# A hybrid pool/RWKV-7 layer: the slots of its round re-sequenced, matrix pieces grouped in threes, and work around the round moved

## The chip, the cores and the metric

One core of one Trainium2 chip runs the kernel. The time is the device time of one execution in microseconds (us). TensorE (PE) multiplies matrices, VectorE (DVE) and ScalarE (ACT) do elementwise work, GpSimd (POOL) does elementwise work and masks, SyncE (SP) issues most transfers. Each engine runs its own list of instructions in order and waits on semaphores.

## The reference, cut to what matters

One layer on 512 tokens of width 1024, all in float32:

```python
mod = silu(c) @ w_ada + b_ada            # sh1, sc1, gt1, sh2, sc2, gt2
h = x * (1 + sc1) + sh1
p = h @ w_in                             # p_pool, p_rwkv, p_gate
y_pool = pool_branch(p_pool, ...)        # means over 2, 4, 8, 16 tokens, a mix, @ w_pool_up
y_rwkv = rwkv7_branch(p_rwkv, ...)       # below
mixed = (g_pool * y_pool + g_rwkv * y_rwkv) @ w_out
x = layer_norm(ALPHA * x + (1 + gt1) * mixed)
f = square(relu((x * (1 + sc2) + sh2) @ w_ff1)) @ w_ff2
x = layer_norm(ALPHA * x + (1 + gt2) * f)
# rwkv7_branch, for each of 16 heads of width 64 and each token in turn:
state = state * decay + (state @ -kk) * (kk * a) + v * k
o = state @ r;  o = layer_norm(o) + bonus * v;  o = o * gate;  y_rwkv = o @ w_rwkv_up
```

## The kernel before

Every large product is made in three terms: weights and activations are split into a high part (ACT, `split_hi`) and the remainder (POOL, `split_lo`), and PE adds high by high, high by low and low by high. A weight chunk of 1024 by 128 columns takes 24 matmuls of 512 columns. `w_hi` and `w_lo` are a ring of two chunks until the rounds are done, so a chunk is split only when the product two chunks before is finished.

**Prologue.** SP loads sixteen tiles of `w_ada`, the token tile, fifteen rows of parameters and the first two weight chunks. DVE adds the tiles up weighted by silu(c) (`acc`, L973 to L976), PE turns the sums into columns (L1404) and `mod` is their value. Then `hf`, its high part and its low part are made tile by tile (L995, L648, L998, L560) and PE does the first five chunks (L1426).

**Rounds.** The recurrence is done in chunks of 64 tokens as matrix products (with an inverse made by squaring), four heads at a time, so in four rounds (`QUADS`). `it` runs from -1 to 4: round `it` works on four heads (`work`), prepares the next four (`prep`, not in `it` 3 and 4) and finishes the four before (`tail`, `it` 1 to 4). A round has 27 slots (`SLOTS`). In each slot every engine does what `slot(it, s)` names, in order. PE's small products (64 by 64 blocks) go to three PSUM sets in the order of `PE_ORDER`, set = place in the list modulo 3; `wait_set_free` makes a product wait until the one before it in its set has been read. Between them PE does pieces of the weight products that go on all the while: a piece is four matmuls (`gemm_piece`), a chunk six pieces, `PER_SLOT` says how many follow the small products of a slot, 36 to a round, in 26 of the 27 slots.

The names that matter below. AT0, AT1, TV, AD0, AD1, A2T, A4, A4T, D1, KR0, KR1, A8T, D2, W0, D, K, HD0, HD1, V1, K2, TT, AP, MR, N, OI are steps of the recurrence; S1 to S6 carry the state from chunk to chunk, one in each of the slots 21 to 26, each waiting for DVE's addition of the one before (L1241). `lora`, `norm` and `inv` (twice a round, 0 and 1) prepare the next heads: ACT's `lora_tanh`, the square root of `norm_root` (L702), DVE's `norm_inverse` (L1075, L1078), PE's `inverse_norm` (L1564), DVE's `unit_keys`, `keys`, `scaled_reads`, `scaled_writes`. The tail normalises `O` over each head: mean (L1152), centring (L1161), square (ACT, L787), sum (L1166), root (ACT, L791), division (L1187), then PE turns it (`yT`), ACT scales it into `y` (L823), DVE adds the bonus (L1210) and multiplies by the gate (L1212, `y_ready`), for which PE makes `gate` (L1591, L1592). ACT needs a table load of its own between square roots and exponentials or tanh. In each round eight more tiles of `w_ada` come through ACT's queue to one place (`ada_tile`), at the slots `ADA_LOADED`, and DVE adds them up at the end of the slots `ADA_USED` (L1249); PE makes `mod` of the sum in the next round. An ACT issue waits until DVE has used up the tile before.

**After the rounds.** The last two gate products of group 3 and the pool mixing (L1765) run while the up-projections' first chunk is loaded, then the up-projections, gates, `w_out`, the first layer norm, four quarters of the feed-forward, the last layer norm.

Of the kernel before, what the change touches and what calls it, by code (L numbers as in the profile page):

```python
# [5 lines left out]
P = 128  # L6
# [7 lines left out]
def build(nc, x, c, w_ada, b_ada, w_in, mu_shift, pool_mix, pool_scale, w_pool_up, w0, w_decay_up, a0,  # L14
# [30 lines left out]
    with ctx:  # L45
# [157 lines left out]
        def over16(m):  # L203
# [5 lines left out]
                    "D1", "KR0", "KR1", "A8T", "D2", "W0", "inv0", "bonus", "D", "lora1", "K", "HD0", "HD1", "yT", "norm1", "gate",  # L209
# [223 lines left out]
        def _(sp):  # L433
# [11 lines left out]
            for q in range(2 * KT):  # L445
# [30 lines left out]
            for k in range(K_UP, K_FF + 2 * KT):  # L476
# [21 lines left out]
        def _(pool):  # L498
# [99 lines left out]
            for k in range(K_UP, K_H2):  # L598
# [1298 lines left out]
```

## Time and profile before

| | |
|---|---|
| time, 3 runs | 1108.73 us median, 1107.64 to 1111.6 |
| profiled execution | 1109.78 us, its span 1108.0 us |
| mean granted TensorE clock | 0.957 of full |
| busy, share of the span | PE 91%, DVE 47%, ACT 37%, POOL 37% |
| prologue, up to the first wide matmul | 0 to 42.4 us |
| rounds -1, 0, 1, 2, 3, 4 begin at | 71.4, 118.9, 210.7, 312.6, 415.1, 511.4 us |
| rounds end | 534.5 us |
| first feed-forward product begins | 726.9 us |

The span runs from the first to the last instruction; the execution's own time is a little longer. Busy PE includes the time in which it runs at the lower of its two clocks.

### The profile page before, as it was taken

What the parts mean: (1) busy time and instruction counts of PE and PEld (TensorE: products, weight loads), DVE (VectorE), ACT (ScalarE), POOL (GpSimd) and SP (SyncE); (2) the same over time, 40 slices, a digit from 0 to 9 for tenths busy, and PEclk for the clock granted to TensorE, in tenths of its full rate; (3) what the DMA queues carried; (4) which work ended last, traced back from release to release, by engine and by line L of the source; (5) the groups of instructions that cost most, each with busy time, mean ns of one, the idle gap of its engine ahead of it and who ended that gap; (6) DMA issues with size and microseconds to landing.
All of it is one profiled execution on the core that took longest, in us unless ns stands there. A gap on an engine that the chain in (4) does not pass through costs nothing.

```text
span 1108.0 us, 25424 instructions
## 1 busy us (share of the span) xinstructions
PE 1008.7 (91%) x10997; PEld 799.2 (72%) x10997; DVE 522.0 (47%) x620; ACT 408.5 (37%) x496; POOL 407.6 (37%) x236
## 2 busy tenths in 40 slices
PE   1898999879988999899899999889999999999992
PEld 1676777666766677677588888768888888888881
DVE  6636578558846775753332155846112112112217
ACT  0345354336234522433532233475224224214311
POOL 7333412402320141123454453436444444444422
PEclk9798999889999998899999999979999999999996
DMA  9322333312432342333334443304323332333201
GB/s 373 101 77 62 97 101 89 91 57 85 114 87 64 98 116 61 96 85 96 116 97 116 135 125 110 93 20 122 106 85 98 105 95 87 102 95 88 84 1 76
DMA packets 153641, 108.08 MB, mean 98 GB/s; under 512 B 5395, under 2 KB 145601, under 8 KB 153537
## 3 DMA queue, kind: packets, MB, share of 16 engines
q1 hardware_dynamic: 143729, 83.46, 25.7%
q10 hardware_dynamic: 9808, 23.08, 7.1%
q8 instruction: 84, 1.38, 0.5%
q14 instruction: 20, 0.16, 0.0%
HBM read 100.23 MB, written 2.10 MB: 92 GB/s over the span
## 4 chain that ended last, share of the span: by engine, by line
PE 76%; DVE 13%; ACT 3%; DMA 2%; issue 2%; POOL 1%; SPq 1%; ACTq 0%; DVEq 0%; POOLq 0%
PE set L1742 23%; PE bank L1742 20%; PE bank L1445 13%; PE set L1499 3%; PE set L1487 3%; PE set L1511 3%; PE set L1523 2%; PE bank L1426 1%; DVE y L1249 1%; PE bank L1844 1%; DVE Q L1020 1%; DMA ptab<-in_mu_shift_dram 1%; DVE Q L1039 1%; PE set L1564 1%; PE set L1534 1%
## 5 line engine op out<-in xcount | busy, mean ns | idle before, releaser
L552 POOL TENSOR_TENSOR w_lo<-w_raw,w_hi 128x1024 fp32r<-128x1024 f32 (+2 forms) x87 | 201.3, 2313 | 443.7 <-ACT w_hi L633 403.6
L608 POOL TENSOR_TENSOR w_lo<-w_raw,w_hi 128x1024 fp32r<-128x1024 f32 x48 | 115.8, 2412 | 145.6 <-ACT w_hi L924 145.5
L661 ACT ACTIVATE Q<-set 128x1024 f32<-128x1024 f32 x56 | 57.4, 1025 | 155.1 <-PE set L1499 83.6
L1445 PE MATMUL bank<-h_hi,w_hi 128*128 128x512 f32 x256 | 110.7, 432 | 0.9 <-issue 0.6
L1445 PE MATMUL bank<-h_hi,w_lo 128*128 128x512 f32 x256 | 108.0, 422 | 0.7 <-issue 0.7
L1445 PE MATMUL bank<-h_lo,w_hi 128*128 128x512 f32 x256 | 108.0, 422 | 0.0
L633 ACT ACTIVATE w_hi<-w_raw 128x1024 fp32r<-128x1024 f32 (+2 forms) x75 | 75.4, 1006 | 81.4 <-PE set L1742 43.5
L924 ACT ACTIVATE w_hi<-w_raw 128x1024 fp32r<-128x1024 f32 x60 | 63.7, 1061 | 110.7 <-PE bank L1742 53.9
L1340 DVE TENSOR_TENSOR f<-t 128x512 f32<-128x512 f32 x32 | 26.4, 825 | 125.5 <-ACT t L933 125.2
L1742 PE MATMUL set<-y_hi,w_hi 128*128 128x512 f32 x192 | 76.1, 396 | 0.0
L1742 PE MATMUL bank<-h_hi,w_hi 128*128 128x512 f32 x192 | 75.8, 395 | 0.0
L1742 PE MATMUL bank<-h_hi,w_lo 128*128 128x512 f32 x192 | 75.3, 392 | 0.0
L1742 PE MATMUL bank<-h_lo,w_hi 128*128 128x512 f32 x192 | 75.2, 392 | 0.0
L1742 PE MATMUL set<-y_lo,w_hi 128*128 128x512 f32 x192 | 75.2, 391 | 0.0
L1742 PE MATMUL set<-y_hi,w_lo 128*128 128x512 f32 x192 | 75.1, 391 | 0.0
L1445 PEld LDWEIGHTS bank<-h_hi,w_lo 128*128 128x128 f32 x256 | 50.5, 197 | 16.5 <-issue 6.2
L1445 PEld LDWEIGHTS bank<-h_hi,w_hi 128*128 128x128 f32 x256 | 50.6, 198 | 15.7 <-issue 4.6
L1445 PEld LDWEIGHTS bank<-h_lo,w_hi 128*128 128x128 f32 x256 | 50.8, 198 | 12.0 <-issue 2.3
L1742 PE MATMUL bank<-y_hi,w_hi 128*128 128x512 f32 x128 | 50.8, 397 | 0.0
L1742 PE MATMUL bank<-y_hi,w_lo 128*128 128x512 f32 x128 | 50.2, 392 | 0.0
L1742 PE MATMUL bank<-y_lo,w_hi 128*128 128x512 f32 x128 | 50.1, 392 | 0.0
L1499 PEld LDWEIGHTS set<-Q 64*64 64x64 f32 x2560 | 41.6, 136 | 11.1 <-issue 9.9
(325 smaller groups left out, 2026.9 us busy)
## 6 DMA issues: line engine op xcount, KB each, us to landing
w_raw<-in_w_ff_dram SPq DMA_DIRECT2D x64, 512.0 KB, 3.9
w_raw<-in_w_in_dram SPq DMA_DIRECT2D x46, 512.0 KB, 3.9
y<-in_w_ada_dram ACTq DMA_DIRECT2D x32, 512.0 KB, 3.8
ada<-in_w_ada_dram SPq DMA_DIRECT2D x16, 512.0 KB, 9.4
w_raw<-in_w_rwkv_up_dram SPq DMA_DIRECT2D x8, 512.0 KB, 3.9
w_raw<-in_w_out_dram SPq DMA_DIRECT2D x8, 512.0 KB, 3.8
xtok<-in_x_dram SPq DMA_DIRECT2D x4, 512.0 KB, 9.7
Q<-Q ACTq DMA_DIRECT2D x16, 128.0 KB
```

The source lines that it names most:

```text
L552: link(pool.tensor_tensor(part_of(k, w_lo), part_of(k, w_raw), part_of(k, w_hi).bitcast(F32), ALU.subtract), "lo_ready")
L608: again(pool.tensor_tensor(part_of(k, w_lo), part_of(k, w_raw), part_of(k, w_hi).bitcast(F32), ALU.subtract), "lo_ready")
L633: link(act.activation(part_of(k, w_hi), part_of(k, w_raw), ACT.Copy), "hi_ready")
L661: link(act.activation(by_half(tile), psum_flat(set_of(name)), ACT.Copy), "act_kept")
L924: link(act.activation(part_of(k, w_hi), part_of(k, w_raw), ACT.Copy), "hi_ready")
L1340: link(dve.tensor_tensor(f3[:, :], r[:, :], r[:, :], ALU.mult))
L1445: mm = pe.matmul(o, w, hx, start=(m == 0), stop=(m == 3 * KT - 1))
L1487: mm = pe.matmul(ps[C * q:C * q + C, p, c * C:(c + 1) * C], by_head(left, p, q, c), by_head(right, p, q, c - back), start=(m == 0), stop=( ...
L1499: mm = pe.matmul(ps[N * p:N * p + N, q, c * C:(c + 1) * C], by_pair(left, p, q, c), by_pair(right, p, q, c), start=(m == 0), stop=(m == le ...
L1511: mm = pe.matmul(ps[C * q:C * q + C, p, 2 * c * C:2 * (c + 1) * C], by_head(left, p, q, HC * h + c), two_blocks(x, z, rows, q, HC * h + c) ...
L1523: mm = pe.matmul(ps[N * p:N * p + N, q, 2 * c * C:2 * (c + 1) * C], by_pair(left, p, q, HC * h + c), two_blocks(x, z, rows, p, HC * h + c) ...
L1742: mm = pe.matmul(o, w[chunks[k][1]][:, kt, :], hx[:, kt, :], start=(kt == 0 and m == 0), stop=(kt == kts - 1 and m == 2))
```

## The change

Nothing is computed in another way. What moves:

- `PER_SLOT` puts the 36 pieces of a round as ten groups of three and six single ones; round -1 has a list of its own (`FIRST_SLOTS`). The small products do not change their order but for `gate`, which goes ahead of `yT`; so `gate` takes the set of number 2, `yT` 0, `norm1` 1.
- The tail: `mod` is added at slot 2 and not after AT1's masks at slot 3; square, variance and root go from slots 4 and 5 to 8 and 9, the division from 8 to 10, and the squares go to the place of `At` and not `b7`.
- `scaled_writes(n, 1)` goes from slot 20 to slot 18, ahead of the additions of MR0 and MR1.
- The eight tiles of `w_ada` come at other slots and through two places, `y` and the block `c1`.
- Prologue: parameters two to a tile, chunk loads ahead of the last two tiles of `w_ada`, the parameters' work and the first half of `mod` between DVE's two sums, and the first two chunks' products side by side, tile by tile.
- After the rounds: the first two up-projection chunks and the mixing weights are loaded earlier, `split_hi(K_UP)` comes later on ACT; at the first layer norm DVE centres the next tile before it sums up, POOL's last split goes behind the low parts, and DVE makes the first low part.

```diff
-                    "D1", "KR0", "KR1", "A8T", "D2", "W0", "inv0", "bonus", "D", "lora1", "K", "HD0", "HD1", "yT", "norm1", "gate",
+                    "D1", "KR0", "KR1", "A8T", "D2", "W0", "inv0", "bonus", "D", "lora1", "K", "HD0", "HD1", "gate", "yT", "norm1",
...
-        ADA_LOADED = (1, 5, 8, 11, 14, 17, 19, 21)
-        ADA_USED = (4, 7, 10, 13, 16, 18, 20, 26)
+        ADA_LOADED = (1, 5, 7, 9, 11, 12, 14, 15)
+        ADA_USED = (4, 8, 10, 11, 13, 14, 16, 18)
+        def ada_tile(kt):
+            return flat_blocks(c1) if kt in (2, 4, 6) else y[:, KT - 2:KT, :].rearrange("p g t -> p (g t)")
+        def ada_before(kt):
+            return (0, 1, 1, 2, 3, 4, 5, 6)[kt]
...
-        PER_SLOT = [1, 1, 1, 2, 2, 1, 1, 2, 1, 1, 1, 2, 1, 1, 0, 2, 1, 3, 3, 1, 2, 1, 1, 1, 1, 1, 1]
+        PER_SLOT = [0, 3, 0, 3, 3, 0, 3, 0, 3, 0, 3, 0, 3, 0, 0, 3, 0, 3, 3, 0, 1, 1, 1, 1, 1, 1, 0]
         LAST_SLOTS = [2, 2, 2, 1, 1, 1, 1, 1, 1] + [0] * 18
+        FIRST_SLOTS = [0, 3, 0, 3, 0, 0, 3, 0, 3, 0, 0, 0, 3, 6, 0, 3, 0, 3, 3, 3, 3, 0, 0, 0, 0, 0, 0]
...
-                if 2 <= q < 2 + len(rows):
-                    tab, at, src = rows[q - 2]
+                for tab, at, src in rows[2 * (q - 2):2 * (q - 1)] if q >= 2 else ():
...
+                if q in (2 * KT - 4, 2 * KT - 3):
+                    load_chunk(sp, q - (2 * KT - 4))
...
-            sp.wait_ge(sem("y_ready"), QUADS)
+            wait_made(sp, "O", QUADS)
+            load_chunk(sp, K_UP)
+            wait_made(sp, "yT", QUADS)
...
+            load_chunk(sp, K_UP + 1)
+            sp.wait_ge(sem("y_ready"), QUADS)
...
-            for f in range(KT):
+            for f in range(1, KT):
...
+            split_lo(K_H2 - 1)
...
+                if s == 9 and tail:
+                    act.wait_ge(sem("o_var"), it)
+                    link(act.activation(gn[:, 2, :], gn[:, 1, :], ACT.Sqrt), "o_std")
+                if s == 8:
...
+                    if tail:
+                        act.wait_ge(sem("centred"), it)
+                        link(act.activation(flat_blocks(At), flat(O), ACT.Square), "o_squared")
...
+                    if it or ada_before(kt):
+                        act.wait_ge(sem("ada2_used"), KT * it + ada_before(kt))
+                    if kt == 2:
+                        wait_made(act, "D1", it)
...
+                if q == KT:
+                    modulation_in()
...
+                    if s == 18 and prep:
+                        scaled_writes(n, 1)
+                if s == 2 and tail:
...
+                    link(dve.tensor_tensor(mod[:, cols], pset[set_of("mod")][:, 0, 0:KT], params[:, cols], ALU.add), "mod2")
...
+                if s == 9 and tail:
+                    dve.wait_ge(sem("o_squared"), it)
+                    link(dve.tensor_reduce(gn[:, 1, :], blocks(At), AX_X, ALU.add))
...
+                if f == 1:
+                    dve.wait_ge(sem("h2_hi"), 1)
+                    link(dve.tensor_tensor(h_lo[:, 0, :], f1[:, :], h_hi[:, 0, :].bitcast(F32), ALU.subtract), "h2_lo_first")
...
+            modulation_columns(0, bank[1])
...
+            modulation_columns(1, bank[7])
+            for f in range(4, 6):
+                turn_x(f)
...
+            for kt in range(KT):
...
+                for k in range(2):
+                    for m in range(3 * kt, 3 * kt + 3):
...
                 if s == 13:
                     if tail:
+                        out_gate(it)
                         pe.wait_ge(sem("o_normed"), it)
                         to_heads("yT", it, [(O, IB)])
                     if prep:
                         norm(it, 1)
-                if s == 14 and tail:
-                    out_gate(it)
```

## Rows read from the trace of the kernel before

**Rows 1.** The page: busy us (share of the span) and instructions of each engine

```profile
PE 1008.7 (91%) x10997; PEld 799.2 (72%) x10997; DVE 522.0 (47%) x620; ACT 408.5 (37%) x496; POOL 407.6 (37%) x236
```

**Rows 2.** Waits of PE, whole span: who waited for whom, us in total, times, longest

```profile
PE set L1487 <- ACT norms L702: 7.5, 2, 3.7
...
PE set L1564 <- DVE inverse L1078: 6.2, 2, 4.7
PE set L1487 <- DVE mod L1151: 6.0, 3, 2.1
PE set L1534 <- DVE Q L1241: 4.4, 2, 2.8
...
PE set L1844 <- POOL h_lo L603: 3.9, 1, 3.9
...
PE set L1499 <- DVE O L1187: 2.2, 1, 2.2
```

**Rows 3.** Rounds -1 to 3: length, busy us of PE, PEld, DVE, ACT, POOL, granted clock, DMA

```profile
71.40:118.90 47.50, 42.78 (x205) 32.64 (x203) 29.27 (x38) 22.70 (x28) 17.29 (x8) 0.93 0.26 70
118.90:210.70 91.80, 83.93 (x1921) 65.06 (x1920) 61.93 (x70) 41.31 (x47) 25.92 (x11) 0.96 0.36 101
210.70:312.60 101.90, 92.48 (x2064) 70.61 (x2063) 69.45 (x82) 44.12 (x51) 24.18 (x10) 0.97 0.32 88
312.60:415.10 102.50, 92.82 (x2065) 70.87 (x2064) 69.39 (x81) 44.05 (x51) 24.10 (x10) 0.97 0.31 86
415.10:511.40 96.30, 89.34 (x2005) 68.92 (x2004) 56.82 (x76) 33.95 (x37) 19.72 (x8) 0.93 0.33 91
```

**Rows 4.** The same columns, a stretch just behind a wait in round 1

```profile
227.30:230.70 3.40, 3.40 (x8) 2.40 (x8) 0.14 (x1) 1.02 (x1) 0.00 (x0) 0.51 0.24 57
```

**Rows 5.** PE in order of time, three pieces in round 1: start, us, operation

```profile
278.86 0.50 PE L1445 MATMUL bank<-h_hi,w_hi 128*128 128x512 f32 x1
279.20 0.40 PE L1445 MATMUL bank<-h_lo,w_hi 128*128 128x512 f32 x1
...
281.53 0.39 PE L1445 MATMUL bank<-h_hi,w_lo 128*128 128x512 f32 x1
281.85 1.16 PE L1499 MATMUL set<-Q 64*64 64x64 f32 x64
```

**Rows 6.** Round 1 in order of time: from yT to the gated y

```profile
269.94 1.59 ACT L823 ACTIVATE y<-set,params 128x512 f32<-128x512 f32 x2 [0.67 <-PE set L1499]
...
271.54 1.28 ACT L702 ACT_TABLE_LOAD   x1
...
273.56 1.22 DVE L1210 TENSOR_TENSOR y<-y,xvb 128x1024 f32<-128x1024 f32 x1
```

**Rows 7.** Round 1 in order of time: DVE and ACT ahead of lora_tanh(1)

```profile
239.99 1.22 DVE L1166 TENSOR_REDUCE gn<-Q 128x16 f32<-128x1024 f32 x1
...
258.58 1.23 DVE L1194 TENSOR_TENSOR xvb<-set,xvb 128x1024 f32<-128x1024 f32 x1 [0.55 <-PE set L1582]
...
262.86 1.29 DVE L1249 SCALAR_TENSOR_TENSOR y<-y,derived 128x1024 f32<-128x1024 f32 x1
...
264.69 0.69 ACT L694 ACTIVATE sg<-set,derived 128x512 f32<-128x512 f32 x1 [2.29 <-DVE y L1249]
```

**Rows 8.** First layer norm in order of time

```profile
717.12 2.34 POOL L552 TENSOR_TENSOR w_lo<-w_raw,w_hi 128x1024 fp32r<-128x1024 f32 x1 [7.76 <-ACT w_hi L633]
...
717.83 1.65 DVE L1316 TENSOR_SCALAR small<-small 128x4 f32<-128x4 f32 x1
```

**Rows 9.** Prologue in order of time

```profile
29.51 6.83 PE L1404 MATMUL bank<-ones_col,acc 128*128 128x1 f32 x32
...
31.28 1.06 ACT L633 ACTIVATE w_hi<-w_raw 128x1024 fp32r<-128x1024 f32 x1 [27.58 <-DMA w_raw<-in_w_in_dram]
...
33.06 1.06 ACT L633 ACTIVATE w_hi<-w_raw 128x1024 fp32r<-128x1024 f32 x1 [0.72 <-DMA w_raw<-in_w_in_dram]
```

**Rows 10.** After the rounds, in order of time

```profile
545.42 1.06 ACT L633 ACTIVATE w_hi<-w_raw 128x1024 fp32r<-128x1024 f32 x1 [7.88 <-DMA w_raw<-in_w_rwkv_up_dram]
```

More of the change, by code:

```diff
@@ L1163, in slot @@
                         decay_sums(n, 0)
-                if s == 5 and tail:
-                    dve.wait_ge(sem("o_squared"), it)
-                    link(dve.tensor_reduce(gn[:, 1, :], blocks(b7), AX_X, ALU.add))
-                    link(dve.tensor_scalar(gn[:, 1, :], gn[:, 1, :], 1.0 / N, GN_EPS, ALU.mult, ALU.add), "o_var")
                 if s == 6:
@@ L1183, in slot @@
                         keep_plus_one(b5, "A8T", "A8T", it)
-                    if tail:
-                        dve.wait_ge(sem("o_std"), it)
-                        link(dve.reciprocal(gn[:, 3, :], gn[:, 2, :]))
-                        link(dve.tensor_tensor(blocks16(O), blocks16(O), gn[:, 3, :].unsqueeze(2).to_broadcast([P, 16, N]), ALU.mult), "o_normed")
                 if s == 9:
@@ L1229, in slot @@
                 if s == 20 and prep:
-                    scaled_writes(n, 1)
                     for q in range(2):
@@ L1301, in _, with first_centre @@
             link(dve.tensor_copy(sum1, res[:, 0, :]))
-            for n in range(1, KT):
+            def first_centre(n):
                 dve.wait_ge(sem("res_ready"), n + 1)
                 link(dve.tensor_tensor(res[:, n, :], res[:, n, :], m0[:, :], ALU.subtract))
+            first_centre(1)
+            for n in range(1, KT):
                 take_product(n)
+                if n < KT - 1:
+                    first_centre(n + 1)
                 if n < KT - 1:
@@ L1390, in turn_x, with modulation_columns @@
                 mm.then_inc(sem("x_turned"), 1)
-            pe.wait_ge(sem("x_in"), 16 * TB)
-            for f in range(4):
-                turn_x(f)
+            def modulation_columns(half, o):
+                pe.wait_ge(sem("ada_used"), KT * (half + 1))
+                for f in range(KT):
+                    mm = pe.matmul(o[:, f:f + 1], acc[:, half, f * P:(f + 1) * P], ones_col[:, :], start=True, stop=True)
+                mm.then_inc(sem("mod_done"), 1)
+            pe.wait_ge(sem("ones_ready"), 1)
+            modulation_columns(0, bank[1])
             pe.wait_ge(sem("params_in"), 16 * 15)
@@ L1399, in _ @@
             mm.then_inc(sem("param_cols"), 1)
-            pe.wait_ge(sem("ones_ready"), 1)
-            for half in range(2):
-                pe.wait_ge(sem("ada_used"), KT * (half + 1))
-                for f in range(KT):
-                    mm = pe.matmul(bank[1][:, 8 * half + f:8 * half + f + 1], acc[:, half, f * P:(f + 1) * P],
-                                   ones_col[:, :], start=True, stop=True)
-            mm.then_inc(sem("mod_done"), 1)
-            for f in range(4, KT):
+            pe.wait_ge(sem("x_in"), 16 * TB)
+            for f in range(4):
+                turn_x(f)
+            modulation_columns(1, bank[7])
+            for f in range(4, 6):
                 turn_x(f)
@@ L1414, in terms_of @@
                 return in_bank(k)[0:width, :], w[slot_of(k)][:, kt, 0:width], hx[:, kt, :]
-            for k in range(5):
+            pe.wait_ge(sem("lo_ready"), 2)
+            for kt in range(KT):
+                pe.wait_ge(sem(("h_lo_by_dve", "h_lo_by_pool")[kt % 2]), kt // 2 + 1)
+                for k in range(2):
+                    for m in range(3 * kt, 3 * kt + 3):
+                        o, w, hx = terms_of(k, m)
+                        mm = pe.matmul(o, w, hx, start=(m == 0), stop=(m == 3 * KT - 1))
+                    if kt == KT - 1:
+                        mm.then_inc(sem("w_used"), 1)
+                if kt < 2:
+                    turn_x(6 + kt)
+            for k in range(2, 5):
                 pe.wait_ge(sem("lo_ready"), k + 1)
```

95 lines of the change are left out of this document (44 added, 51 removed).

## The prediction

> **What bounds the kernel now.** The page comes first: PE is busy 91% of the span, all others under half [rows 1]. So only two things can shorten it, PE's idle time and what PE is busy with beyond its work: starts of segments, and time at the lower clock. PE's waits, one by one, say where the idle time is [rows 2]: two waits of 3.7 us for the square root of `norm_root`, two for the inverse norm (4.7 in round -1, 1.5 in round 0), three of 2.1 for `mod`, two in the state steps (2.8 in round 0, 1.6 in round 1), 3.9 ahead of the feed-forward, 2.2 for the last `yT`. The windows by round give the sums that the change has to be set against, with the granted clock: 0.93 in rounds -1 and 3, 0.96 to 0.97 between [rows 3]. A stretch behind one of the waits runs at 0.51, the lower of the two levels, for 3.4 us and gives half of its work [rows 4]; so a wait of over 2 us mostly costs 1.7 us more than itself. In round 3, 0.93 over 96.3 us is 14% of it at the lower clock, 6.7 us lost; in round -1 3.3.
>
> I price the change by walking through each slot in the new order with the durations of before. All sums are against the profiled execution's 1109.8 us; the median of the runs is 1.05 us under it.
>
> **Pieces in threes.** A segment of twelve matmuls takes 2.99 us: 0.34 to its second, 0.32 from its last to the next small product, and (281.53 - 279.20) / 10 = 0.233 between [rows 5]. So each segment costs (0.34 + 0.32 - 2 x 0.23) = 0.2 us beyond its matmuls. A round has 16 segments in place of some 25: 9 x 0.2 = 1.8 us less, 7 us over four rounds.
>
> **Round -1.** The list puts six pieces between `norm1` and `inv1`, where one stood. A piece is 0.93 us, so five more (4.7) cover the 4.7 wait, and the low clock behind it goes (3.3). The six added to covers elsewhere are taken from the end, where POOL has to make its two scaled blocks before TB; that comes out even. With 1 us kept back: **-7**.
>
> **Round 0.** The state-step wait came from DVE's `scaled_writes`, `rt` products and an `ada` tile ahead of L1241. `scaled_writes` goes to slot 18, where DVE has three pieces of slack. 2.8 goes to about 1.6 (ACT's flips still delay the projection at slot 22, and one piece less stands ahead of it), the low clock behind it goes (0.04 x 91.8 = 3.7), segments 1.8; against it, `norm1` and `inv1` now stand without a piece between, so the 1.5 wait grows by a piece to 2.2 or 2.4: **-5** after some small waits (BR0 for TB's copy, HD1 for the tanh).
>
> **Rounds 1 and 2.** Gone: 2.1 for `mod` (it is added before the masks), 3.7 for `norm_root` (the tail's root no longer stands ahead of it), segments 1.8, and the low clock behind both, 0.03 x 102 = 3.1. New, and the heart of this prediction:
> - *HD1.* ACT's `lora_tanh(1)` already waited 2.29 for DVE to use up an `ada` tile [rows 7]. DVE's stretch from the bonus product to the end of that tile is 264.15 - 258.58 = 5.6 us. Into it come the sum (1.22 and a small one), the reciprocal and the division (the size of the sum): 3.0 us, so 8.6. Bonus itself comes two pieces later after PE's A8T. And ACT has a root in slot 9, so tanh needs a table load of 1.28 [rows 6] that it did not need before. HD1 shares its set with `lora1`: PE reaches HD1 about 17 us after A8T, the tanh is done after 21: a wait of 4.
> - *inv1.* `gate` now has set 2, and the next in set 2 is `inv1`, so PE waits there for `y_ready`, not only for the inverse. From the end of `yT`: 0.2, two scalings 1.59, table load 1.28, root 0.2, inverse 0.4, two DVE passes of 1.22 [rows 6]: 6.2 us. PE has only `norm1`, 0.9, to put against it: a wait of 5.3.
> - Behind these two waits 1.7 us of clock each, and in round 1 the state-step wait goes from 1.6 to 2.5.
> Sum: round 1 gives up 10.7 and takes 14 to 15: **+4**; round 2, where slot 22 has no projection, **+1**.
>
> The Trainium skill (ScalarE: Activation LUTs, What ACT_TABLE_LOAD costs) speaks against the change here: it puts a switch of function sets at 2.66 us, 1.28 of load and 1.38 of drain. The row shows 1.28, and ACT's next instruction starts right behind it; I take the row. By the page the two waits would be about 1.4 us longer each, in two rounds some 5 us on the sum.
>
> **Round 3** has no preparation, so neither new wait. The waits for `mod` and for the variance ahead of KR go, two or three low stretches with them. Small content and 36 pieces come to 80 us, waits for D's copy behind the root 1.8, for y's scaling before V1 1.9, hiccups 1.5: 85 against 96.3 [rows 3], **-11**.
>
> **Round 4 and after.** `gate` (4.1 us of PE) covers the chain to the division: the wait of 2.2 [rows 2] and the slow stretch behind it go, -3. The first up-projection chunk no longer comes at 545.4 [rows 10]; ACT's queue gets past it, and two waits at the pool mixing go: -2. Together **-5**.
>
> **Prologue.** The work for `mod`'s first half leaves the end of the chain: half of 6.83 [rows 9], -3.4. But the chunk loads now stand ahead of the last two tiles; one chunk lands 1.8 us behind the other [rows 9], so the last tile lands 3.6 later. And POOL then splits both chunks while DVE still adds tiles: beside a split of 2.34 a DVE instruction on four columns took 1.65 [rows 8], so each split may hold DVE for up to 2.3. That gives 0 to +4 at `hf`. The two chunks side by side start 1 to 2 us earlier and wait less for tiles, but both end together, so the third chunk's copy, split and low part (2 us) are no longer covered. Bounds 0 to +5; I take **+3.5**, since the splits fall on the additions.
>
> **First layer norm.** POOL's split is no longer ahead: 1.65 to 0.17, -1.5 [rows 8]; the first low part by DVE -0.7. **-2.5** with the clock. Reordering the centring leaves the same operations ahead of the last sum: nothing.
>
> Sum: -7 - 5 + 4 + 1 - 11 - 5 + 3.5 - 2.5 = -22, so 1088 for the profiled execution, and **1087** for the median.
>
> **The rivals.** *The new waits are half what I make them* (DVE ahead of my walk, PE behind it, each hiding the other): half of twice (4 + 5.3 + 3.4) = 13 us off, 1075. For it: the old DVE was idle a third of the round [rows 3]. Against: both are chains of fixed lengths.
> *Most is lost again:* the chains that I find in two rounds bite in rounds 0 and 3 too, or collisions of POOL with DVE on the new path, a few at 2.3 each: +12, 1099.
> *Nothing comes of it,* because round 3 keeps its waits (11) and the prologue loses 5 or more: 1107.
> *Slower.* With pieces in threes there are long stretches of 64-column products alone, up to 6 us. Should these be granted the lower clock, each costs 1.7 us in 3.4. It decides from about 15 such stretches more than I count, three to four a round: then 1115. In its favour, the first tiles of `mod` in round 3 are followed by the low level with hardly a wait ahead. Against: rounds 1 and 2 have such stretches of 4 us now at a mean clock of 0.97. The Trainium skill (TensorE: Matmul & The Clock Gate, HAM oscillation) says that a kernel can lose the clock again at every wait of a loop; the low stretch behind a wait agrees [rows 4].
>
> **How the numbers follow.** The forecast's own range is 1080 to 1096, 0.58. Half waits 0.18; mostly lost 0.12; nothing 0.06; slower 0.06. Under 1073 and over 1103 I leave 0.2 in all, most of it above. A difference of 0.5%, 5.5 us, is what a measurement tells from none. Faster: 0.58 + 0.18 + 0.12 - 0.02 = 0.86; same 0.07; slower 0.07.
>
> **What would show it.** In rounds 1 and 2 a wait of about 4 at HD1 for ACT's tanh and one of about 5 at L1564 for DVE's gate multiplication (L1212 of before), no wait at TV or D1; no wait at `inv1` in round -1; round 3 near 85 us; rounds 1 and 2 not shorter. Wrong it would be if DVE's work of slots 9 and 10 were held further by collisions, if the clock fell in stretches without a wait, or if the chunk loads cost the prologue more than 5.

## The result: 0.34% slower, where 2% faster was forecast

The changed kernel takes 1113.61 us (median of 20 runs, 1106.94 to 1118.47) beside 1108.74 us for the kernel before in the same runs: a ratio of 1.0034, 95% interval 1.0019 to 1.0048. The forecast was 1087, range 1073 to 1103. The profiled execution took 1113.02 us, its span 1111.3.

Busy time of each engine, from the page of the changed kernel:

```profile
PE 996.6 (90%) x10997; PEld 800.9 (72%) x10997; DVE 523.9 (47%) x621; ACT 413.8 (37%) x500; POOL 402.9 (36%) x235
```

PE has the same instructions and is busy 12 us less than before [rows 1]; that is the part that worked. It idles 15 us more, so the gain is more than spent on waiting. Its waits, in the changed kernel (who waited for whom, us in total, times, longest):

```profile
PE bank L1426 <- DVE acc L1007: 13.4, 1, 13.4
PE set L1426 <- DVE acc L1007: 13.4, 1, 13.4
PE set L1604 <- DVE y L1236: 10.7, 2, 5.3
PE set L1539 <- issue: 8.9, 10, 1.9
PE set L1563 <- ACT aa_odd L707: 7.6, 3, 3.7
PE set L1539 <- DVE Q L1064: 6.2, 3, 2.5
PE set L1883 <- DVE h_lo L1357: 3.3, 1, 3.3
PE set L1574 <- DVE Q L1264: 3.2, 2, 1.9
...
PE set L1527 <- issue: 2.7, 3, 1.1
PE set L1539 <- DVE O L1220: 2.5, 1, 2.5
...
PE set L1527 <- ACT y L836: 1.8, 1, 1.8
```

L1604 is `inverse_norm`, L1563 HD1, L1574 the state steps, L1426 the columns of `mod` in the prologue. Against [rows 2]: the waits for `mod` and for `norm_root` are gone, and the one of 4.7 in round -1 is 1.6. In their place stand the two that were forecast, 3.7 at HD1 and 5.3 at `inv1`, in each of rounds 1 and 2. And there is a line that was not forecast: waits on "issue", for nothing that the profile shows. All of these on PE, in any line, sum to 14.0 us in 16 pauses; before they summed to 7.9 in ten.

Not all of them are of one kind. Number everything that PE's trace records, in order: matmuls, weight loads, semaphore and register instructions. Before, all ten pauses stand at numbers that leave 193 to 195 when divided by 256. In the changed kernel twelve of the 16 leave 193 or 194; these sum to 10.0 us. The other four (1.87, 0.80, 0.80 and 0.45 us) stand elsewhere, and each ends within 0.1 us of the end of an operation by which ACT or DVE writes `Q`; I read them as waits for data that the profile did not name. So the pauses that repeat every 256 instructions grew by some 2 us over the whole kernel, and not by 6; in round 3 alone they grew from 1.3 to 5.8.

By round (us, busy of PE, PEld, DVE, ACT, POOL, granted clock, DMA share and GB/s; rounds -1, 0, 1, 2, 3, and last the stretch behind the wait at HD1 in round 1):

```profile
75.40:117.30 41.90, 39.93 (x205) 30.58 (x203) 28.77 (x38) 22.72 (x28) 16.48 (x7) 1.00 0.29 79
117.30:205.30 88.00, 80.47 (x1917) 64.65 (x1918) 62.34 (x69) 41.36 (x47) 25.38 (x12) 0.98 0.36 103
205.30:314.70 109.40, 93.45 (x2064) 73.59 (x2064) 68.96 (x81) 46.72 (x53) 23.79 (x10) 0.92 0.30 84
314.70:420.20 105.50, 90.74 (x2068) 71.84 (x2068) 68.23 (x80) 46.63 (x53) 24.10 (x10) 0.95 0.28 79
420.20:516.90 96.70, 85.31 (x2012) 68.08 (x2008) 60.13 (x76) 34.74 (x39) 19.57 (x8) 0.96 0.33 92
257.60:264.40 6.80, 5.47 (x40) 4.39 (x41) 5.67 (x6) 4.31 (x5) 0.00 (x0) 0.50 0.31 102
```

Round -1 lost its low clock (0.93 to 1.00) and 5.6 us, round 0 lost 3.8 us. Round 1 is 7.5 longer and round 2 3.0 longer, both at a lower mean clock than before (0.92 and 0.95 beside 0.97 [rows 3]), for the clock falls to its lower level behind each of the new waits. Round 3, where 11 us were to be gained, is as long as before.

### The profile page after: what moved, and what is told of

Same layout as the page of the kernel before. It is cut to its first block, busy times and chain, and to the rows that moved or that the text cites. A ratio compares the mean times of both kernels' runs of the same rounds, so it can differ in the third digit from the quotient of the medians.

```text
span 1111.3 us, 25426 instructions
## 1 busy us (share of the span) xinstructions
PE 996.6 (90%) x10997; PEld 800.9 (72%) x10997; DVE 523.9 (47%) x621; ACT 413.8 (37%) x500; POOL 402.9 (36%) x235
## 3 DMA queue, kind: packets, MB, share of 16 engines
q8 instruction: 84, 1.38, 0.5%
## 4 chain that ended last, share of the span: by engine, by line
PE 45%; DVE 5%; ACT 1%; issue 0%; POOL 0%; DVEq 0%; ACTq 0%; POOLq 0%
PE set L1781 22%; PE bank L1781 20%; PE bank L1883 1%; DVE G L1327 1%; DVE aa L1335 1%; DVE t L1312 1%; PE set L1883 1%; DVE xt L1404 1%; DVE xt L1406 1%; DVE G L1316 0%; PE set L1845 0%; PE set L1862 0%; DVE stat L1364 0%; PE set L1769 0%; DVE O L1220 0%
## 5 line engine op out<-in xcount | busy, mean ns | idle before, releaser
L1485 PE MATMUL bank<-h_lo,w_hi 128*128 128x512 f32 x256 | 103.3, 404 | 0.0
L1485 PE MATMUL bank<-h_hi,w_lo 128*128 128x512 f32 x256 | 102.5, 400 | 0.0
L1781 PE MATMUL set<-y_hi,w_hi 128*128 128x512 f32 x192 | 75.8, 395 | 0.4 <-POOL w_lo L563 0.4
L1781 PE MATMUL bank<-h_hi,w_lo 128*128 128x512 f32 x192 | 75.5, 393 | 0.0
L1781 PE MATMUL bank<-h_lo,w_hi 128*128 128x512 f32 x192 | 75.4, 393 | 0.0
L1781 PE MATMUL set<-y_lo,w_hi 128*128 128x512 f32 x192 | 75.2, 391 | 0.0
L1539 PE MATMUL set<-Q 64*64 64x64 f32 x2560 | 45.7, 223 | 16.0 <-issue 8.9
```

The lines of the kernel that those rows point to most:

```text
L1485: mm = pe.matmul(o, w, hx, start=(m == 0), stop=(m == 3 * KT - 1))
L1539: mm = pe.matmul(ps[N * p:N * p + N, q, c * C:(c + 1) * C], by_pair(left, p, q, c), by_pair(right, p, q, c), start=(m == 0), stop=(m == le ...
L1781: mm = pe.matmul(o, w[chunks[k][1]][:, kt, :], hx[:, kt, :], start=(kt == 0 and m == 0), stop=(kt == kts - 1 and m == 2))
```

## The experiments

Lengths of the stages in every kernel that computes the layer, from its profiled execution, in us; a stage ends where PE's first product of the next begins. The numbers of a single execution scatter by 2 us a stage and more, since stretches at the lower clock come and go: round 3 of e2_old_slots has a granted clock of 0.91, that of the changed kernel 0.96.

| kernel | prologue | -1 | 0 | 1 | 2 | 3 | 4 | to the feed-forward | rest | ratio to before, 95% interval |
|---|---|---|---|---|---|---|---|---|---|---|
| before | 71.4 | 47.5 | 91.8 | 101.9 | 102.5 | 96.4 | 23.1 | 192.4 | 381.2 | 1 |
| changed | 75.4 | 41.9 | 88.0 | 109.4 | 105.4 | 96.8 | 22.4 | 190.9 | 381.0 | 1.0034 (1.0019 to 1.0048) |
| e1_gate_back | 75.4 | 41.9 | 90.6 | 102.5 | 99.7 | 90.6 | 30.4 | 191.0 | 380.2 | 0.9965 (0.9942 to 0.9988) |
| e2_old_slots | 76.0 | 41.9 | 92.0 | 104.3 | 103.7 | 100.0 | 21.6 | 191.1 | 380.2 | 1.0049 (1.0031 to 1.0066) |
| e3_slots_only | 71.4 | 41.9 | 91.3 | 106.1 | 105.4 | 95.7 | 25.6 | 193.9 | 381.2 | 1.0050 (1.0027 to 1.0073) |
| e5_tanh_first | 75.2 | 41.9 | 95.1 | 105.4 | 102.5 | 97.3 | 22.4 | 193.2 | 381.3 | 1.0034 (1.0017 to 1.0051) |
| e6_chunks_late | 73.5 | 41.9 | 88.9 | 108.8 | 105.7 | 97.2 | 22.4 | 193.2 | 381.3 | 1.0018 (0.9992 to 1.0045) |
| e7_combined | 71.7 | 41.9 | 96.2 | 96.8 | 94.0 | 94.3 | 22.4 | 193.4 | 381.2 | 0.9849 (0.9819 to 0.9879) |
| e8_old_slots_gate_back | 75.8 | 41.9 | 92.6 | 100.5 | 98.1 | 95.8 | 27.3 | 191.1 | 380.2 | 0.9931 (0.9905 to 0.9957) |
| e9_combined_late | 72.2 | 41.9 | 90.7 | 97.9 | 96.8 | 91.7 | 22.5 | 191.8 | 381.3 | 0.9822 (0.9797 to 0.9847) |
| e10_combined_old_slots | 71.8 | 41.9 | 91.3 | 94.1 | 98.2 | 97.2 | 22.1 | 192.3 | 380.8 | 0.9852 (0.9820 to 0.9884) |
| e11_round_4 | 71.7 | 41.9 | 90.6 | 98.2 | 95.8 | 94.2 | 19.1 | 199.9 | 381.2 | 0.9851 (0.9829 to 0.9874) |
| e12_narrow_split | 72.0 | 41.9 | 88.4 | 98.0 | 94.8 | 94.5 | 22.2 | 192.8 | 380.4 | 0.9790 (0.9768 to 0.9813) |

### Gate moved back

```diff
-                    ..., "HD0", "HD1", "gate", "yT", "norm1",
+                    ..., "HD0", "HD1", "yT", "norm1", "gate",
-                        out_gate(it)                     # slot 13
...
+                if s == 14 and tail:
+                    out_gate(it)
```

> The changed kernel with gate behind norm1 again, as before (order of the sets and of the code; the mixing weights are loaded after y_ready again, which that order needs). My theory: the 5.3 us at inv1 in rounds 1 and 2 is the wait for y_ready through the shared set, so it goes, with the low clock behind it: 7 to 8 us less in each of the two rounds; in round 3 the 1.8 us ahead of V1 goes; round 4 gets longer by the cover of the gate product, 4 to 5 us. In sum about 11 us less than the changed kernel, so near 1102. Rival: the chain of ACT and DVE behind yT is the limit whatever stands in the set; then a wait of 4 to 5 us comes back at K2 or at inv1 for the inverse, and the time stays within 3 us of the changed kernel.

Measured: 1105.47 us beside 1109.59 for the kernel before. That is 0.7% under the changed kernel when both are set against before, some 8 us where 11 were expected. The theory holds for the wait: it goes, and does not come back at `inv1` or K2. These rows of the changed kernel show the wait that is undone (start, us, engine, line, operation):

```profile
273.89 0.17 DVE L1095 TENSOR_SCALAR norms<-norms 128x8 f32<-128x8 f32 x1 [9.56 <-ACT norms L714]
274.09 0.20 DVE L1098 RECIPROCAL inverse<-norms 128x8 f32<-128x8 f32 x1
274.33 1.23 DVE L1234 TENSOR_TENSOR y<-y,xvb 128x1024 f32<-128x1024 f32 x1
...
275.59 1.22 DVE L1236 TENSOR_TENSOR y<-y,set 128x1024 f32<-128x1024 f32 x1
...
276.96 1.98 PE L1604 MATMUL set<-ident,inverse 128*64 128x128 f32 x16 [5.34 <-DVE y L1236]
```

The inverse that `inverse_norm` multiplies is there at 274.3, and PE starts only when DVE has read `gate` out of the shared set, at 276.8: 2.5 of the 5.3 us belong to the set alone. With `gate` behind `norm1` its 4.1 us of products cover the rest too, and no wait is left there. The windows of rounds 1, 2 and 3 of this kernel:

```profile
207.90:310.40 102.50, 91.89 (x2065) 72.27 (x2064) 68.77 (x81) 46.73 (x53) 23.03 (x10) 0.95 0.31 88
310.40:410.10 99.70, 89.79 (x2064) 70.66 (x2064) 68.02 (x80) 46.64 (x53) 22.78 (x10) 0.97 0.29 83
410.10:500.70 90.60, 83.54 (x2014) 66.51 (x2013) 59.32 (x76) 34.79 (x39) 19.07 (x8) 0.98 0.36 98
```

They are 6.9, 5.7 and 6.2 us shorter than with `gate` first. For rounds 1 and 2, 7 to 8 each were expected. Round 4 pays 8.0 where 4 to 5 were expected: `yT` waits 6.5 us there, 4.0 more than with `gate` first, and more of the round runs at the lower clock. Of round 3 only the 1.8 at V1 (for ACT's scaling of `y`) were expected; with them go a stretch at the lower clock and, though no piece has moved, 3.1 us of the pauses that repeat with the block of 256 (5.8 to 2.7).

### The slots of before, in the changed kernel

```diff
-        PER_SLOT = [0, 3, 0, 3, 3, 0, 3, 0, 3, 0, 3, 0, 3, 0, 0, 3, 0, 3, 3, 0, 1, 1, 1, 1, 1, 1, 0]
+        PER_SLOT = [1, 1, 1, 2, 2, 1, 1, 2, 1, 1, 1, 2, 1, 1, 0, 2, 1, 3, 3, 1, 2, 1, 1, 1, 1, 1, 1]
```

> The changed kernel with the PER_SLOT of before in rounds 0 to 3 (FIRST_SLOTS kept). My prediction's step: threes save 0.2 us at each of 9 segments in a round, so undoing them costs 7 us, 1121. Rival (instruction supply): the waits that the trace ascribes to nothing ('issue') sum to 14.1 us in the changed kernel and 8.2 before and sit 256 instructions of PE apart, behind long runs of 64-column products; with the old slots they fall back to about 8, so the 7 is mostly cancelled and the time is within 3 us of 1113.6.

Measured: 1113.91 us, ratio 1.0049, no different from the changed kernel's 1.0034. The waits on "issue" fall from 14.0 to 9.9 us. So threes bring nothing here in sum. Where the seven us went that I had put down for them is worked out behind e10_combined_old_slots.

### The new slots alone, in the kernel before

```diff
-        PER_SLOT = [1, 1, 1, 2, 2, 1, ...]
+        PER_SLOT = [0, 3, 0, 3, 3, 0, ...]
...
+        FIRST_SLOTS = [0, 3, 0, 3, 0, 0, 3, 0, 3, 0, 0, 0, 3, 6, 0, 3, 0, 3, 3, 3, 3, 0, 0, 0, 0, 0, 0]
```

> The kernel before with the new PER_SLOT and FIRST_SLOTS alone. Prediction's step: round -1 5.6 to 7 us shorter, rounds 0 to 3 1.8 each, with the waits for mod and norm_root still there: 1096. Instruction supply: round -1 the same, but 'issue' waits of PE rise from 8.2 to about 14: 1101 to 1104. Third: the old tail's waits grow, since the singles that covered them are gone, and it is no faster than before.

Measured: 1113.73 us, 0.5% slower than before, although round -1 gives its 5.6 us. Rounds 1 and 2 grow by 4.2 and 2.9. The first expectation, 1096, is wrong by 18 us; the second, 1101 to 1104, by 10 or more; the third holds. The waits on "issue" are 14.9 us, all at the repeating place in the block, and waits of 2.0 to 2.4 appear at `inv0` in rounds 0, 1 and 2 (its set is that of A8T, which DVE has still to copy); single pieces had covered them.

### Instruction supply by itself

```python
piece(64); narrow(2048)                      # wide: 128x128 by 512 columns; narrow: 64x64 by 64, fp32
for _ in range(8):  piece(12); narrow(192)
for _ in range(24): piece(4);  narrow(64)
for _ in range(4):  piece(12); narrow(384)
```

> The suspected cost by itself: no layer is computed, only 64-column products of 64 rows in fp32, 2048 in a row, then 8 times 12 wide matmuls and 192 narrow ones, then 24 times 4 wide and 64 narrow, then 4 times 12 wide and 384 narrow, with no semaphore between them. Instruction supply: pauses of about 1 us that stand 256 instructions (128 matmuls) apart; in the row of 2048 at nearly every such place, in the 192s at some, with 64s at none or small ones. Rival (no such thing; the 'issue' waits come from semaphores that the trace doesn't show): no pause anywhere, one pitch throughout, and the 8 x (12 + 192) take less than the 24 x (4 + 64) by 16 segment starts of 0.2 us.

A narrow product in fp32 stands as two records, so `narrow(64)` is 128. The kernel ran once. Windows of the four parts (the counts are matmuls, and each has a weight load beside it):

```profile
22.36:138.35 115.99, 66.86 (x4098) 62.64 (x4097) 0.00 (x0) 0.00 (x0) 1.00 0.02 5
138.35:233.20 94.85, 74.00 (x3174) 64.83 (x3168) 0.00 (x0) 0.00 (x0) 1.00 0.02 4
233.20:324.10 90.90, 82.26 (x3175) 66.30 (x3168) 0.00 (x0) 0.00 (x0) 1.00 0.02 5
324.10:417.60 93.50, 61.94 (x3128) 55.86 (x3120) 0.00 (x0) 0.00 (x0) 1.00 0.02 4
```

In order of time, one of the pauses in the first part, and from the page the queue that brings instructions:

```profile
100.33 1.39 PE L53 MATMUL set<-raw 64*64 64x64 f32 x79 [1.64 <-issue]
```

```profile
q8 instruction: 106, 1.74, 1.7%
```

There is no semaphore in these parts. In the first part, behind a first one of 1.12, pauses of 1.36 to 1.91 us stand exactly 128 matmuls apart, which is 256 instructions with the loads, and 106 transfers of 1.74 MB are 16 KB each. The first part takes 116 us for 32 such blocks: **3.6 us for a block**, where the products alone take 2. The second and third part hold the same products, and the second starts 16 segments fewer; a group of four wide ones takes 1.13 us and one of twelve 2.95, so a start costs 0.22 and the second part should be 3.5 us shorter. It is 4.0 longer: bunching costs it 7.5 us of supply. In the third part the pauses are small, 0.1 to 0.8 us but for one of 1.34. All 83 "issue" pauses of this kernel leave 193 when their number is divided by 256, as those of the layer leave 193 to 195: that is why I take the twelve in the changed kernel for the supply of instructions.

The Trainium skill (Runtime: NRT & Kernel Launch, Instruction fetch mechanics) says that instructions come in blocks of 256; the spacing of the pauses agrees. It also says that crossing from one block to the next is mostly hidden. With products as short as these it is not: the row shows 1.64 us.

The rival for "slower" in my prediction, that long stretches of narrow products are granted the lower clock, falls: the first window is 116 us of nothing else at a clock of 1.00.

### ACT's issue out of the way of the tanh

```diff
-        ADA_LOADED = (1, 5, 7, 9, 11, 12, 14, 15)
+        ADA_LOADED = (1, 5, 7, 9, 12, 13, 14, 15)
```

> The changed kernel with two tiles of w_ada issued a slot later (ADA_LOADED 11, 12 become 12, 13), so that ACT no longer stands at an issue, waiting for DVE's use of a tile, ahead of lora_tanh(1). My theory: the tanh then starts right behind the squares and its table load, 2.3 us earlier; the wait at HD1 in rounds 1 and 2 goes from 3.7 to about 1.4 and with it a stretch at the lower clock: 2.3 to 4 us in each of the two rounds, 5 to 8 in sum, about 1107 against 1113.6. Rival: the tanh waits for PE's lora or for the root of the tail whatever ACT issues, then HD1 keeps at least 3 us and nothing changes; or the tile now comes too late for DVE's slot 13 and the wait is found again at inv1.

The rows of the changed kernel that the edit aims at, ACT ahead of the tanh in round 1:

```profile
253.14 0.72 ACT L696 ACTIVATE G<-G,params 128x512 f32<-128x512 f32 x1
255.73 0.34 ACTq L863 DMA_DIRECT2D Q<-in_w_ada_dram  x1
256.17 1.28 ACT L706 ACT_TABLE_LOAD   x1 [2.31 <-DVE y L1272]
257.47 0.69 ACT L706 ACTIVATE sg<-set,derived 128x512 f32<-128x512 f32 x1
258.19 0.69 ACT L707 ACTIVATE aa_odd<-set,derived 128x512 f32<-128x512 f32 x1
...
258.93 1.99 PE L1563 MATMUL set<-Q 64*64 64x128 f32 x32 [3.68 <-ACT aa_odd L707]
```

Measured: 1114.16 us, ratio 1.0034, nothing gained in sum. The mechanism is right: the wait at HD1 is 1.39, and rounds 1 and 2 are 4.0 and 2.9 shorter, although the wait at `inv1` grows from 5.3 to 5.8. The second rival is right too, in round 0, which is 7.1 longer:

```profile
169.84 2.34 POOL L563 TENSOR_TENSOR w_lo<-w_raw,w_hi 128x1024 fp32r<-128x1024 f32 x1 [14.83 <-ACT w_hi L645]
170.08 3.18 DVE L1272 SCALAR_TENSOR_TENSOR y<-Q,derived,y 128x1024 f32<-128x1024 f32 x1 [1.86 <-DMA Q<-in_w_ada_dram]
...
173.76 1.98 PE L1604 MATMUL set<-ident,inverse 128*64 128x128 f32 x16 [5.66 <-DVE inverse L1098]
```

The tile lands late, DVE waits 1.9 us for it and then takes 3.18 us for an addition that takes 1.28 by itself, since POOL splits a chunk beside it; the inverse is queued behind, and PE waits 5.7 for it.

### Chunk loads behind the last tiles

```diff
-                if q in (2 * KT - 4, 2 * KT - 3):
-                    load_chunk(sp, q - (2 * KT - 4))
+            for k in range(RING):
+                load_chunk(sp, k)
```

> The changed kernel with the first two weight chunks loaded behind the last tiles of w_ada, as before, and nothing else. Theory: two of DVE's additions took 3.2 us in place of 1.28 because POOL split the chunks beside them; they come back to 1.3, and hf starts 3.5 to 4 us earlier than 42.1 us. The 3.75 us by which DVE's second sum starts later than before, waiting for the parameters' transposes, stays. 1113.6 becomes about 1110. Rival: the split only moves into the hf products and costs the same there, so the first wide product starts within 1 us of where it does.

Measured: 1112.29 us, ratio 1.0018 (0.9992 to 1.0045), not to be told from the changed kernel, where 3.6 us less were expected. `hf` starts at 40.0 against 42.1, so 2.1 earlier and not 3.5 to 4, for one addition still runs beside a split. In the changed kernel, four additions of which two are held (start, us over all four):

```profile
27.70 9.18 DVE L1007 SCALAR_TENSOR_TENSOR acc<-ada,derived,acc 128x1024 f32<-128x1024 f32 x4
...
29.39 6.41 POOL L563 TENSOR_TENSOR w_lo<-w_raw,w_hi 128x1024 fp32r<-128x1024 f32 x2 [6.44 <-ACT w_hi L645]
```

and in this kernel, two of which one is held:

```profile
31.32 4.75 DVE L1007 SCALAR_TENSOR_TENSOR acc<-ada,derived,acc 128x1024 f32<-128x1024 f32 x2
...
32.64 5.64 POOL L563 TENSOR_TENSOR w_lo<-w_raw,w_hi 128x1024 fp32r<-128x1024 f32 x2 [9.62 <-ACT w_hi L645]
```

DVE's second sum starts at 24 us, some 3.5 later than before, in both: it stands behind the copies of the parameters, whose transposes come on PE behind the columns of the first half.

### Three edits undone or moved, together

Gate first in round 4 alone; the tiles as in e5_tanh_first; the prologue of before.

```diff
-        pe_items = [(name, it) for it in range(-1, QUADS + 1) for name in PE_ORDER if runs(name, it)]
+        pe_items = [(name, it) for it in range(-1, QUADS) for name in PE_ORDER if runs(name, it)]
+        pe_items += [(name, QUADS) for name in ("O", "mod", "gate", "yT")]
...
```

> Gate behind norm1 in rounds 1 to 3 but ahead of yT in round 4, the two tiles of w_ada a slot later, and the prologue of before; the rest as changed. If the terms add up: 1105.5 of the run with gate moved back, 4 less for the prologue, 4 to 8 less in round 4, 5 to 8 less at HD1: about 1090. Rival: waits behind each other, so that what one edit frees is lost at the next place (the state steps, the additions of MR); then 1098 or more.

Measured: 1093.16 us, 1.5% faster than before. Rounds 1 and 2 take 96.8 and 94.0 and round 4 22.4; round 0 keeps the wait of 5.7 us of e5_tanh_first, which the sum of 1090 did not hold. With it, 4 us more than it was before that edit, the terms add up.

### The slots of before, with gate moved back

> The changed kernel with both PER_SLOT and gate as before, so what is left of the round's change is the tail's later steps, the tiles of w_ada and scaled_writes. If threes are worth what the prediction said, it is 7 us slower than the run with gate alone moved back (1105.5), so 1112. If segment starts saved and instruction supply lost cancel, as the run with the old slots alone says, it is within 3 us of 1105.5, with the 'issue' waits of PE summing to less than 10.5 us.

Measured: 1100.82 us, ratio 0.9931, beside 0.9965 for its pair with threes. It comes out below both expectations by 1 to 2 us or more; the "issue" waits sum to 9.1. Threes look 0.3% worse here, though the two intervals (0.9905 to 0.9957 and 0.9942 to 0.9988) still overlap.

### The tiles' use moved as well, and its pair with the slots of before

```diff
-        ADA_LOADED = (1, 5, 7, 9, 12, 13, 14, 15)
-        ADA_USED = (4, 8, 10, 11, 13, 14, 16, 18)
+        ADA_LOADED = (1, 5, 7, 9, 12, 13, 15, 16)
+        ADA_USED = (4, 8, 10, 11, 14, 15, 17, 18)
```

> The combined kernel (1093.2) with DVE's use of the late tiles moved behind the inverse norm too: ADA_LOADED (1, 5, 7, 9, 12, 13, 15, 16), ADA_USED (4, 8, 10, 11, 14, 15, 17, 18). In the combined kernel round 0 took 96.2 us, with 5.7 us at inv1, where DVE stood at slot 13 for a tile that landed late and then ran beside a split of POOL. Theory: that wait goes back to 1.4 us as in the changed kernel, round 0 to about 90, the HD1 waits of rounds 1 and 2 stay at 1.4: near 1087. Rival: tiles used that late push DVE's additions ahead of MR and the state steps, which each wait about 2 us already; then rounds 1 and 2 give the gain back.

> The same with the PER_SLOT of before in rounds 0 to 3: pieces one by one. The pair with gate moved back gave 1105.5 with threes and 1100.8 with the old slots. If threes cost that (starts of segments saved, less instruction supply and covers lost), this is 3 to 5 us faster than its pair, near 1083. If the pair was chance or the covers differ here, both agree within 2 us; if threes gain what I predicted, it is 7 slower.

Measured: 1089.00 and 1093.76 us, ratios 0.9822 and 0.9852. The first is as expected: round 0 goes back to 90.7 with 1.07 at `inv1`. Rounds 0 to 3 of e9_combined_late:

```profile
114.10:204.80 90.70, 82.32 (x1917) 66.32 (x1918) 61.54 (x69) 41.35 (x47) 25.08 (x12) 0.96 0.36 103
204.80:302.70 97.90, 89.04 (x2068) 69.77 (x2066) 68.12 (x81) 46.74 (x53) 22.93 (x10) 0.98 0.32 92
302.70:399.50 96.80, 88.58 (x2064) 70.17 (x2062) 67.32 (x80) 46.64 (x53) 22.74 (x10) 0.98 0.30 86
399.50:491.20 91.70, 82.67 (x2016) 65.35 (x2015) 59.32 (x76) 34.81 (x39) 19.04 (x8) 1.00 0.35 97
```

The second was to be 3 to 5 us faster and is 4.8 slower, its interval overlapping that of the first. So my reading of the pair before it as a fixed price falls. Four pairs now say what threes do to the time in rounds 0 to 3: -0.15% (changed against e2), +0.34% (e1 against e8), -0.30% (e9 against e10), and in the kernel before about +1% (e3, with the 5.6 us of round -1 taken out). The first three are at the edge of what these runs can tell from nothing; the fourth, in a kernel whose waits the single pieces covered, is a loss.

The saving at the starts is there all the same. Two rounds that ran at the full clock from end to end, round 1 of e10_combined_old_slots with single pieces and round 2 of e7_combined with threes:

```profile
204.90:299.00 94.10, 89.11 (x2061) 68.16 (x2060) 67.47 (x81) 46.71 (x53) 23.18 (x10) 1.00 0.33 95
306.70:400.70 94.00, 87.13 (x2070) 68.72 (x2068) 67.88 (x80) 46.62 (x53) 23.51 (x10) 1.00 0.32 90
```

PE is busy 2.0 us less with threes, near the 1.8 forecast, and the round is as long. Over rounds 0 to 3 of the profiled executions (us, threes less singles; the time lost to the lower clock is taken out of PE's busy time by the granted clock of each stretch):

| pair | busy at full clock | PE idle | of it, pauses of the block | lost to the lower clock |
|---|---|---|---|---|
| e3 and before | -5.7 | +13.4 | +7.0 | -1.7 |
| changed and e2 | -7.0 | +11.3 | +3.0 | -4.7 |
| e1 and e8 | -8.2 | +6.4 | -0.4 | -2.0 |
| e9 and e10 | -5.9 | +3.9 | +1.7 | -1.9 |

So threes earn their 6 to 8 us every time, and more idle time spends most or all of it: some of it the supply of instructions, more of it waits that the single pieces had covered. The clock column is within the scatter of single executions.

### Round 4, and the narrow run of slots 18 to 20

```diff
+                if s == 9 and it == QUADS:       # ACT, ahead of the gate and the split of the slot
...
+                    link(act.activation(gn[:, 2, :], gn[:, 1, :], ACT.Sqrt), "o_std")
...
-                if it == QUADS and s in (2, 5):
+                if it == QUADS and s in (2, 10):
```

> The late combined kernel (1089.0) with, in round 4 alone, ACT's root ahead of the gate and split of slot 9, and three of its copies of y behind the root instead of ahead of the squares. In the changed kernel yT of round 4 waits 2.5 us behind gate's 4.1, so the chain from O to the division had grown by 4 us: 1.9 of it are the three copies, 1.7 the gate and the split, the rest a division that ran beside POOL. Theory: that wait goes and the lower clock behind it: 2.5 to 4 us less, 1085 to 1086.5. Rival: the copies are needed by the up-projections soon after, or the root's table load only moves, and the wait stands at the pool mixing: within 1 us of 1089.

Measured: 1094.27 us, ratio 0.9851 beside 0.9822: no gain, where 2.5 to 4 us were expected, and rather a loss. The wait of `yT` is gone and round 4 is 19.1 in place of 22.5, but the stage behind it is 8.1 longer. The rival is right in kind: PE comes to the pool mixing before its weights, whose load follows `y_ready` and one 512 KB chunk:

```profile
523.10 1.22 PE L1801 MATMUL set<-aa,wmix 128*128 128x512 f32 x1 [5.92 <-DMA wmix<-in_pool_mix_dram]
```

```diff
-        PER_SLOT = [..., 0, 3, 3, 0, 1, 1, 1, 1, 1, 1, 0]
+        PER_SLOT = [..., 0, 3, 1, 2, 1, 1, 1, 1, 1, 1, 0]
```

> The late combined kernel with two of the three pieces of slot 18 in slot 19, so that N and OI, 256 64-column records in a row, have eight wide ones between them. Number of pieces, segments and instructions stay but for one start more (0.2 us a round). Instruction supply: in round 3 the pause of 1.9 us in that run goes to under 0.7, in round 1 and 2 the same run's waits (0.7 and 1.6; 2.5, put down to DVE) shrink by 1 to 2 each: 3 to 6 us less, about 1085. Rival: the pause belongs to OI's own inputs and only moves behind the pieces, or MR0 now waits for AP's copies: no gain.

Measured: 1087.31 us, ratio 0.9790 (0.9768 to 0.9813), the fastest of all and 2.1% under the kernel before; the gain over e9_combined_late, 1.7 us or 0.3% where 3 to 6 us were expected, is within the two intervals. The same instruction (the 16,632nd of PE's matmuls and loads) in both, first with N and OI in one run, then with two pieces between them:

```profile
480.75 0.81 PE L1530 MATMUL set<-Q 64*64 64x64 f32 x40 [1.93 <-issue]
```

```profile
479.12 0.81 PE L1530 MATMUL set<-Q 64*64 64x64 f32 x40 [0.40 <-issue]
```

The pause belongs to the place in the list and to the narrow products ahead of it, not to OI's inputs. But the sum of "issue" waits is 14.6 us beside 13.2: other blocks' pauses grew (the one at 410.7 us from 0.4 to 1.75). What one block was spared, another here paid.

## Why the prediction was wrong, step by step

The forecast stood at -22 us against the profiled execution, and +3 came. By its own terms:

- **Round 3, -11, measured +0.4.** This is the step that failed. It said "small content and 36 pieces come to 80 us", waits of 1.8 for D's copy and 1.9 before V1, hiccups 1.5: 85, with nothing for the lower clock. Set beside the traces (us; busy time with the loss to the lower clock taken out):

| | before | forecast | changed |
|---|---|---|---|
| PE busy, at full clock | 82.9 | 80 | 82.1 |
| lost to the lower clock | 6.6 | 0 | 3.2 |
| pauses that repeat with the block of 256 | 1.3 | 1.5 (all hiccups) | 5.8 |
| other idle time | 5.6 | 3.7 | 5.6 |

  Both waits are there: 1.80 at V1, and 1.87 for D's copy, which the profile puts down to "issue" although PE starts just behind the copy:

```profile
467.81 1.02 ACT L673 ACTIVATE Q<-set 128x1024 f32<-128x1024 f32 x1 [0.41 <-ACT gn L809]
...
468.93 1.76 PE L1539 MATMUL set<-Q 64*64 64x64 f32 x64 [1.87 <-issue]
```

  Half of the clock's loss was won back. The rest of the 11 us rested on three terms: content that was 2.1 too small, no lower clock behind two waits that the sum itself kept (3.2), and hiccups of 1.5 where six pauses of 0.45 to 1.38 stand, 5.8 together; before there were two, of 0.72 and 0.56. The largest two in the changed kernel:

```profile
457.90 0.45 PE L1539 MATMUL set<-Q 64*64 64x64 f32 x12 [1.34 <-issue]
...
506.52 0.81 PE L1539 MATMUL set<-Q 64*64 64x64 f32 x40 [1.38 <-issue]
```

  The first stands at the instruction (14,856th) where the kernel before pauses 0.72. The kernel without layer (e4) shows what it is, and e12_narrow_split moves one. In round 3 the four kernels with single pieces have 1.3 to 2.4 us of such pauses, the nine with threes 2.7 (e1) to 7.2 (e6). In three of the four pairs bunching adds 3 to 5 us of them there, in the fourth, e1 against e8, 0.3: it is behind most of this term, together with the place of `gate`. The stretches at the lower clock stand behind D's copy and around V1's wait; no run takes them away by themselves. Taking `gate` back (e1) removes V1's wait, one of these stretches, 3.1 us of the pauses, and 6.2 us in all.
- **Pieces in threes, -7, counted inside the rounds.** The price of a start was right (0.20 from [rows 5], 0.22 in e4), and so was the saving in PE's busy time (5.7 to 8.2 in four pairs); that it shortens the kernel by as much was not. It left out that single pieces cover waits and space out the narrow products. Measured in time: between -0.3% and +1%.
- **Round 4 and after, -5, and the first layer norm, -2.5: measured -0.7 in round 4 and -1.5 from there to the feed-forward.** At the layer norm the wait ahead of the feed-forward went from 3.9 to 3.3 us. The gate was said to "cover the chain to the division". It covers 4.1 us, but the same change makes that chain 4 us longer: three copies of `y` now stand ahead of the squares (1.9), a gate and a split ahead of the root (1.7), and the division runs beside a split. This is read from the order of the rows; e11_round_4 undoes the first two and the wait goes. The division in the changed kernel, 2.77 us where it took 1.22:

```profile
534.63 2.77 DVE L1220 TENSOR_TENSOR O<-O,gn 128x1024 f32<-128x1024 f32 x1
```

- **Round 1, +4, and round 2, +1: measured +7.5 and +2.9.** The terms written down for round 1 (4, 5.3, twice 1.7, 0.9) add up to 13.6 and not to the "14 to 15" of the sum, so they say +3. And of the "three of 2.1" for `mod`, two are 2.1 and the one of round 3 is 1.7. The mechanisms and prices at HD1 (4, measured 3.7) and `inv1` (5.3, measured 5.3) were right, and e1 and e5 confirm both causes. Mis-sized is what stands behind them: PE is at the lower level until 264.4, 5.5 us of work behind HD1's wait (the last window above), which costs 2.7 and not the 1.7 counted, and much the same behind `inv1`; and the pauses of the block sum to 2.6 us in round 1, where they were 1.6.
- **Round -1, -7, and round 0, -5: measured -5.6 and -3.8.** Right in kind. The wait at `inv1` of round -1 was to be covered whole, and 1.65 is left.
- **Prologue, +3.5: measured +4.0.** Right in size, half right in cause. The splits hold two additions by 2.0 each, as priced. But the tiles' later landing was not what delayed the second sum: it was the parameters' work put ahead of it (3.75 us), which I had counted as a gain alone. Moving the loads back (e6) gives 2 of the 4.

On the rule of the Trainium skill that I set aside (ScalarE: Activation LUTs, What ACT_TABLE_LOAD costs): the trace agrees with the row, 1.28 us from 256.17 and the tanh at 257.47 right behind, and shows nothing of the further 1.38.

Kernels with `gate` and the tiles elsewhere and the prologue of before do come to 1089.0 (e9_combined_late) and 1087.3 (e12_narrow_split). That they lie at the forecast is chance: in e9 rounds 1 and 2 are 4.0 and 5.7 shorter than before, where the forecast had them longer, and round 3 takes 91.7, not 85.

What stays open: what brings the single stretches at the lower clock, and what a given list of pieces will cost in supply. The sum of pauses followed no count that I formed; moving `gate` alone changed it by 3 us in round 3. The best of these lists, e12_narrow_split, is not told from e9_combined_late. The earlier chunk and mixing loads after the rounds were not tried alone.

## What to carry to other kernels

Before you bunch the long instructions of a stream, look for waits on "issue" in the dense runs between them and number them in the engine's whole list, semaphore and register instructions too: those at the same place of a block of 256 are the supply of instructions, and bunching made them longer in three pairs of four here; the others are waits for data. Set what bunching saves in busy time against the waits that the single pieces covered. When an operation moves to another place in a ring of buffers, ask who takes its buffer next and what that one now waits for: 2.5 of the 5.3 us at `inv1` came from the ring alone, and with one reordering rounds 1 and 2 got 12.6 us shorter. Price each moved chain in the last pass too, where the work that used to stand between its steps is different.

## What the runs showed of the hardware

PE gets its instructions in blocks of 256, and with nothing but 64-column products it got one in 3.6 us on average (e4); these products in fp32, at 16 ns a record with a load beside each, use one up in 2 us. The pauses stand at the same place of the block in the layer and in e4. Behind twelve wide products, a run of 384 records in e4 mostly pauses for 1.0 and 1.6 us; runs of 128 behind four wide ones mostly for 0.1 to 0.7. A clock of 1.00 held for 116 us of such products with pauses of up to 1.9 us between them, so neither narrow products nor pauses of that length bring the lower level by themselves.
